# The 16 remaining tokens of a recurrent mixer as one packed block-diagonal system, with its inverse in the turns of the big one

## The reference, cut to what matters

```python
def rwkv7_scan(r, decay, k, v, kk, a):
    def step(S, inp):
        r_t, w_t, k_t, v_t, kk_t, a_t = inp
        sa = jnp.einsum('bhvk,bhk->bhv', S, -kk_t)
        S = (S * w_t[:, :, None, :]
             + sa[..., None] * (kk_t * a_t)[:, :, None, :]
             + v_t[..., None] * k_t[:, :, None, :])
        o = jnp.einsum('bhvk,bhk->bhv', S, r_t)
        return S, o
```

## Time and profile before

| | us |
|---|---|
| three timed runs | 1591.23, 1601.34, 1601.97 |
| their median | 1601.34 |
| the profiled execution's own time | 1596.85 |
| its span in the profile | 1595.1 |
| mean granted clock of TensorE in it | 0.99 |

### The profile page before, as it was taken

One profiled execution on the slowest core, in us unless ns is written; L12 is line 12 of the kernel. 1 busy time (PEld: TensorE's weight loads), 2 busy tenths in 40 slices (PEclk: granted clock), 3 DMA queues, 4 the chain that ended last, 5 costly groups with the idle time before them and its releaser, 6 DMA issues. The chain is left out here.

```text
span 1595.1 us, 33719 instructions
## 1 busy us (share of the span) xinstructions
PE 1521.0 (95%) x14204; PEld 1465.0 (92%) x14204; DVE 1042.8 (65%) x1584; ACT 741.1 (46%) x1025; POOL 61.0 (4%) x82
## 2 busy tenths in 40 slices
PE   5999999999999999999999999999998998899997
PEld 5999998999999898999989998999998987799996
DVE  7999647888763868454488855545445677565644
ACT  2555434696212754444456022566334345466532
POOL 0121100000110000110000100000000000000000
PEclk9999999999999999999999989999999999999999
DMA  9899754543221455555433001344543331235551
GB/s 367 312 331 342 271 195 163 178 166 119 78 86 59 167 207 217 202 194 187 176 127 132 10 29 31 129 167 175 176 168 114 133 115 71 79 137 202 190 187 51
DMA packets 39200, 256.86 MB, mean 161 GB/s; under 512 B 4259, under 2 KB 5668, under 8 KB 9892
## 3 DMA queue, kind: packets, MB, share of 16 engines
q1 hardware_dynamic: 37492, 251.07, 43.6%
q10 hardware_dynamic: 1584, 3.97, 0.6%
HBM read 251.87 MB, written 3.15 MB: 160 GB/s over the span
## 5 line engine op out<-in xcount | busy, mean ns | idle before, releaser
L472 DVE TENSOR_TENSOR w_lo<-raw,w_hi 128x2048 fp32r<-128x2048 f32 (+2 forms) x203 | 456.3, 2248 | 388.4 <-ACT w_hi L464 387.8
L572 PE MATMUL bank<-x_hi,w_hi 128*128 128x256 f32 (+1 forms) x1826 | 519.2, 284 | 15.0 <-DVE w_lo L472 6.1
L464 ACT ACTIVATE w_hi<-raw 128x2048 fp32r<-128x2048 f32 (+2 forms) x203 | 382.0, 1882 | 303.0 <-PE bank L574 281.2
L574 PE MATMUL bank<-x_hi,w_lo 128*128 128x256 f32 (+1 forms) x1826 | 511.5, 280 | 0.0
L573 PE MATMUL bank<-x_lo,w_hi 128*128 128x256 f32 (+1 forms) x1826 | 511.0, 280 | 0.0
L572 PEld LDWEIGHTS bank<-x_hi,w_hi 128*128 128x128 f32 x1826 | 343.3, 188 | 22.7 <-issue 14.9
L573 PEld LDWEIGHTS bank<-x_lo,w_hi 128*128 128x128 f32 x1826 | 343.7, 188 | 0.9 <-issue 0.7
L574 PEld LDWEIGHTS bank<-x_hi,w_lo 128*128 128x128 f32 x1826 | 343.6, 188 | 0.0
L573 PE MATMUL bank<-mh_lo,w_hi 128*128 128x272 f32 (+1 forms) x512 | 144.4, 282 | 0.0
L572 PE MATMUL bank<-mh_hi,w_hi 128*128 128x272 f32 (+1 forms) x512 | 144.4, 282 | 0.0
L574 PE MATMUL bank<-mh_hi,w_lo 128*128 128x272 f32 (+1 forms) x512 | 144.4, 282 | 0.0
(11 more groups left out here) (611 smaller groups left out, 2512.4 us busy)
## 6 DMA issues: line engine op xcount, KB each, us to landing
raw<-in_stream SPq DMA_DIRECT2D x227, 1024.0 KB, 4.8
raw<-in_stream SPq DMA_DIRECT2D x8, 768.0 KB, 4.0
gate_store<-stage ACTq DMA_DIRECT2D x8, 256.0 KB, 2.3
raw<-in_stream SPq DMA_DIRECT2D x4, 512.0 KB, 3.4
h<-in_h ACTq DMA_DIRECT2D x1, 1088.0 KB, 9.8
zt<-gate_store SPq DMA_DIRECT2D x1, 1024.0 KB, 5.7
gate<-gate_store SPq DMA_DIRECT2D x1, 1024.0 KB, 7.9
out<-h SPq DMA_DIRECT2D x8, 128.0 KB, 1.8
```

The costliest lines, as they stand in the source:

```text
L464: nc.scalar.activation(w_hi[:, s_at % 2, 0:kt], raw[:, r_at % RING, 0:kt], ACT.Copy).then_inc(hi_done, 1)
L472: nc.vector.tensor_tensor(w_lo[:, s_at % 2, 0:kt], raw[:, r_at % RING, 0:kt], w_hi[:, s_at % 2, 0:kt].bitcast(F32), ALU.subtract).then_inc ...
L572: nc.tensor.matmul(out, hi, xh[:, k0 + k, 0:L], start=start, stop=False)
L574: mm = nc.tensor.matmul(out, lo, xh[:, k0 + k, 0:L], start=False, stop=stop)
```

## The change

The end chunk's heads are packed. Of each half (partitions 0 to 63 and 64 to 127) the four heads' 16 tokens form one 64x64 system, block-diagonal in blocks of 16 (`ends_*`, tiles of 128x64). A gram of all four heads is one 64x64 product, and masks (`ends_before`, `ends_upto`) keep the blocks. The four levels of its inverse stand in the turns of the big inverse: `begin_ends` behind `grow` of turn 1, then for levels 1 to 3 `ends_p` at the start of turns 2 to 4, `ends_masked`, `ends_y` and, ahead of the big `grow`, `ends_grown`. The instance `small` is gone from the steps, and step 2 becomes `last_step`. TURN_BUSY goes from 4 to 3, SOLVE_BUSY from 3 to 7, and one call of SOLVE_BUSY products is left in the steps; fillers of turns change places (slabs in even ones, bonus in odd ones). `pool_products(3)` moves into step 0. In step 1 the state's products for the outputs go ahead of the wait for the solution, and the new state waits for these alone (`state_read`). `begin_out` now does two tiles in the last step and six behind it. On ACT, `outputs(0)` and `square(0)` come behind `pool_out(2)` and the pooling tiles' high part; on DVE the second w_lo split moves from step 1 to step 0, and `centred(0)`, `variance(0)` shift.

```diff
-TURN_BUSY, FIRST_TURN_BUSY, SOLVE_BUSY, END_BUSY, OUT_BUSY, MIX_BUSY = 4, 12, 3, 8, 14, 26
+TURN_BUSY, FIRST_TURN_BUSY, SOLVE_BUSY, END_BUSY, OUT_BUSY, MIX_BUSY = 3, 12, 7, 8, 14, 26
...
                 shifted(None, 6, 0)
+                dve.wait_ge(q["sh_done"], VAL2 + 1)
+                nc.vector.tensor_copy(v_ends[:].rearrange("p (k n) -> p k n", k=RW), v_t[:, :, 2 * P:T2]).then_inc(q["v_ends"], 1)
                 split_lo(dve, following(S["ev_u"], None, 2, 0, 0, False))
...
+                def ends_of(xs, bank, c0):
+                    for n, x in enumerate(xs):
+                        for ps in HALVES:
+                            mm = nc.tensor.matmul(banks[bank][ps, c0 + 64 * n:c0 + 64 * (n + 1)], ends_left[ps, x % 2], grams[x][1][ps, :, end_cols], start=True, stop=True)
                     mm.then_inc(m["gr2"], 1)
+
+                def ends_p(l):
+                    pe.wait_ge(m["e_x"], l)
+                    for ps in HALVES:
+                        mm = nc.tensor.matmul(banks[0][ps, ENDS_P], ends_a[ps, 0], joined(ends_x[ps], l, 0)[:, 0], start=True, stop=True)
+                    mm.then_inc(m["e_p"], 1)
...
-                        small.products_p(pe, 2 * c)
                         idle_slab(1, SOLVE_BUSY)
...
+                    if c:
+                        pe.wait_ge(m["oo_out"], 1)
+                        for k in range(RW):
+                            mm = nc.tensor.matmul(banks[5][:, k * P:(k + 1) * P], r_t[:, k, cols], state_bd[:, k], start=k == 0, stop=False, skip_group_check=True)
+                        mm.then_inc(m["state_read"], 1)
...
+                def last_step():
+                    pe.wait_ge(m["st_out"], 2)
+                    pe.wait_ge(m["gr2_out"], 1)
+                    for ps in HALVES:
+                        for k in range(RW):
+                            nc.tensor.matmul(banks[0][ps, 0:64], ends_kk[ps, 64 * k:64 * (k + 1)], state_bd[ps, k, ps], start=k == 0, stop=False)
+                        mm = nc.tensor.matmul(banks[0][ps, 0:64], ends_ak[ps, 0], v_rw[ps, 2, 0:64], start=False, stop=True)
+                    mm.then_inc(m["rr"], 1)
+                    begin_out(BEGUN[0:2])
+                    pe.wait_ge(m["e_x"], 4)
+                    pe.wait_ge(m["rr_out"], 3)
+                    for ps in HALVES:
+                        mm = nc.tensor.matmul(banks[1][ps, 0:64], ends_y_t[ps, 0], rhs_r[ps, 0:64], start=True, stop=True)
+                    mm.then_inc(m["ww"], 1)
...
+                    begin_out(BEGUN[2:8])
...
                     else:
+                        if l - 1 in ENDS_LEVELS:
+                            ends_p(l - 1)
                         if l % 2:
+                            bonus_product((l + 1) // 2)
+                        else:
                             idle_slab(0, TURN_BUSY)
-                        else:
-                            bonus_product(1 + l // 2)
                         big.products_p(pe, l)
...
+                    if l - 1 in ENDS_LEVELS:
+                        ends_y(l - 1)
                     if l:
                         big.products_y(pe, l)
...
-                ends_of((0, 1))
+                ends_of((1, 2, 3), 2, 0)
                 big.cross_y(pe)
                 pool_products(1)
-                ends_of((2, 3))
-                idle_slab(1, SOLVE_BUSY)
                 big.wait_whole(pe)
                 step_of(0)
                 step_of(1)
-                begin_out(BEGUN[0:4])
-                step_of(2)
+                last_step()
...
+                def begin_ends():
...
+                    link(dve, "dve", nc.vector.tensor_scalar(ends_a[:, 0], banks[0][:, ENDS_A], -1.0, None, ALU.mult))
+                    nc.vector.tensor_copy(joined(ends_y_t[:], 0, 0), joined(eye, 0, 0))
+                    link(dve, "dve", nc.vector.tensor_tensor(joined(ends_y_t[:], 0, 1), joined(ends_a[:], 0, 1), mask, ALU.mult))
+                    link(dve, "dve", nc.vector.tensor_tensor(joined(ends_y_t[:], 0, 1), joined(eye, 0, 1), joined(ends_y_t[:], 0, 1), ALU.subtract))
+                    nc.vector.transpose(ends_x[:, 0], ends_y_t[:, 0]).then_inc(m["e_x"], 1)
...
+                    if l - 1 in ENDS_LEVELS:
+                        ends_grown(l - 1)
+                    big.grow(dve, l)
+                    if l == 1:
+                        begin_ends()
```

More of the change, by code:

```diff
@@ L2645, in step_of @@
                         pe.wait_ge(m["kb_out"], 4)
[L2646 to L2653, removed]
+                        pool_products(2, 3)
+                        for k in range(3):
+                            first_outputs(k)
@@ L2695, in _ @@
                         pe.wait_ge(act_took, 2 + S["ev_u"].t0 + 2)
+                        pe.wait_ge(m["e_left"], 1)
+                        ends_of((0,), 0, ENDS_A.start)
                         big.products_p(pe, l, (0,))
@@ L2808, in _ @@
                 nc.scalar.activation(x_hi[:, 4:8], z_pool, ACT.Copy).then_inc(m["z_hi"], 1)
+                outputs(0)
+                square(0)
                 root(0)
                 outputs(1)
-                small.diagonal(act)
                 square(1)
@@ L2931, in normed, with ends_masked, ends_grown @@
                     nc.vector.tensor_tensor(heads8(dev[0:C, c]), heads8(dev[0:C, c]), rstd, ALU.mult).then_inc(m["nrm"], 1)
+                def begin_ends():
+                    mask = const("levels").rearrange("p (l f n) -> p l f n", l=LEVELS, f=2)[:, 0, 1][:, None, :, None]
+                    eye = const("eyes")[:, None, :]
+                    dve.wait_ge(m["gr2"], 1)
+                    link(dve, "dve", nc.vector.tensor_scalar(ends_a[:, 0], banks[0][:, ENDS_A], -1.0, None, ALU.mult))
[3 more added lines that the diff above has]
+                    nc.vector.transpose(ends_x[:, 0], ends_y_t[:, 0]).then_inc(m["e_x"], 1)
+                def ends_masked(l):
+                    half, b = QUAD // 2, 1 << l
+                    mask = const("levels").rearrange("p (l f n) -> p l f n", l=LEVELS, f=2)[:, l, 0].rearrange("p (n b) -> p n b", b=b)[:, None]
+                    link(dve, "dve", nc.vector.memset(ends_prod[:], 0.0))
+                    dve.wait_ge(m["e_p"], l)
+                    product = banks[0][:, ENDS_P].rearrange("p (h n b) -> p h n b", h=1, b=b)
+                    nc.vector.tensor_tensor(joined(ends_prod[:], l, 0), product, mask, ALU.mult).then_inc(m["e_pd"], 1)
+                def ends_grown(l):
+                    part = joined(ends_y_t[:], l, 1)
+                    dve.wait_ge(m["e_yu"], l)
+                    link(dve, "dve", nc.vector.tensor_tensor(part, part, banks[1][:, ENDS_P].rearrange("p (h n b) -> p h n b", h=1, b=1 << l), ALU.subtract))
+                    nc.vector.transpose(ends_x[:, 0], ends_y_t[:, 0]).then_inc(m["e_x"], 1)
                 for n, x in enumerate((nb_t[:], k_t)):
@@ L2937, in _ @@
                 nc.vector.tensor_tensor(r_t, r_t, log_g[:], ALU.mult).then_inc(m["decayed"], 1)
+                for n, x in enumerate((nb_t[:], k_t)):
+                    ins = nc.vector.tensor_copy(ends_left[:, n].rearrange("p (k n) -> p k n", k=RW), x[:, :, end_cols])
+                ins.then_inc(m["e_left"], 1)
                 for c in range(2):
@@ L2957, in _ @@
                 rescaled(1)
[L2958 removed]
+                dve.wait_ge(m["e_kz"], 1)
+                nc.vector.tensor_copy(ends_kk[:].rearrange("p (k n) -> p k n", k=RW)[:, :, 0:TAIL], kk_t[:, :, end_cols])
                 dve.wait_ge(m["gr2"], 2)
[L2960 to L2964 removed]
@@ L2966, in small_p @@
-                def small_p(l):
-                    small.zero(dve, nc.vector, l)
-                    small.masked(dve, l)
+                for n, (dst, mask) in enumerate(((ends_ak, "ends_before"), (ends_rb, "ends_upto"), (ends_rk, "ends_upto"))):
+                    ins = nc.vector.tensor_tensor(dst[:, 0], banks[2][:, 64 * n:64 * (n + 1)], const(mask), ALU.mult)
+                ins.then_inc(m["gr2_out"], 1)
                 for c in range(2):
                     right_side(c)
-                    small_p(2 * c)
```

168 lines of the change are left out of this document (69 added, 99 removed).

## The result

The changed kernel took 1611.6 us (median of 20 runs, 1600.2 to 1616.7), the kernel before in the same comparison 1594.2 (20 runs, 1586.1 to 1613.2). The ratio on record is 1.0098, with a 95% interval of 1.0078 to 1.0119 (the medians divided give 1.011): slower, where 1582 was forecast and 1595 was the upper end. The profiled execution took 1612.4 us, of which 1610.6 are span.

What follows compares the result with a forecast made beforehand. PE, busy 95% of the span, was taken as the bound, with a PE-DVE loop setting the turns. Profiled 1596.85 us, +3.5 before step 0, -18.3 from there to the next stage gave 1582.0; range 1574 to 1595.

Steps and rivals of the forecast that it cites:

- Turn 2: Start of the big inverse's second turn: PE's new wait for DVE's ends_x delays the big product, +2.5 us (+1.5 to +3.2).
- the sum: Whole kernel: profiled 1596.85 us, +3.5 up to step 0, -18.3 from there to the next stage, giving 1582.0.
- step 0: First step after the turns: products, seven slabs, transposes and state at full clock, 11.3 us where it was 13.8.
- Rival (c): Turns: clock falls in the wait and isn't given back while only 64-row products run; +24, 1606 us; chance 0.06.
- only cover: Turns: the four slabs at 901.97 merely fill PE's time while DVE's loop sets the turn of 6.89 us.
- Rival (b): Turn 2: PE waits and the clock falls for half a turn; +2 to +4, about 1585 to 1586 us; chance 0.14.
- The turns: Turns 2 to 4: small subtraction and transpose lengthen DVE's loop; 7.3 or 7.5 us a turn, +0.6, +0.4, +0.5.
- Rival (d): Turns: small inverse's DVE operations meet full queues, +6 not +3.5, and steps gain only 13.3; 1589.6 us; chance 0.10.
- The steps: Step 0 to the next stage at full clock: 38.5 us where it was 56.8, so -18.3.
- rival (a): Steps: the clock falls there all the same, PE's chain losing about 5 us; 1587 us; chance 0.22.
- the gain from alternating halves: Step 2: overlapping both halves would make the first ten products 0.7 us instead of 1.4; not taken in the forecast.

Runs made afterwards that it cites:

- the version with the product behind: The changed kernel with the small product (ends_x, ends_a) behind the big one in turns 2 to 4, so without the wait: 1576.3 us, ratio 0.9908.
- the run with five copies: The kernel before plus only a PE wait ahead of turn 2 for five small DVE copies behind turn 1's second transpose: 1625.9 us, ratio 1.0223.
- the gap covered: The changed kernel with 21 more slab products in turn 2 ahead of the wait for ends_x: 1579.2 us, ratio 0.9918.
- the run with 40 slabs: The changed kernel with 40 slab products instead of 3 at the start of turn 4: 1597.2 us, ratio 1.0031.

## Why the prediction was wrong

*The step that failed* is "Turn 2", the +2.5 us for the first new wait, together with the price of the clock in it. The wait was seen, in its place, with its releaser, and nearly in its size: idle 2.69 us for a forecast of about 2.4, a delay of 2.9 us by itself for 2.5. What failed is the sum's premise that everything behind it keeps its durations, so that the fall of the clock stood in the sum at nothing. From the second product to step 0 it took 63.91 us where the forecast's terms give 37.67, +26.2, and step 0 took 16.58 us (959.74 to 976.32) for a forecast 11.3, +5.3. Together that is 31.5 us; the profiled execution missed the 1582.0 by 30.4. Rival (c) named this mechanism with a price of +24, though it took the half clock to end with the 64-row products, where it went on through most of step 0. It got a chance of 0.06.

*The argument against rival (c)* was that the same turns ran at full clock with four slabs a turn, and that PE is busy again right after the gap. Both are true, and neither bears on the question. That full clock is kept in a stretch says nothing of whether it is given back there; 75.00 us of 75 busy at 0.50 show that it isn't. And the slabs, "only cover" in the prediction, were no spare help: without them and with 0.73 us of idle time in their place the clock goes.

*Rival (b) and the page behind it.* The Trainium skill, "TensorE: Matmul & The Clock Gate", Part 1, section "What's actually happening", has the clock fall after an idle spell and return after a busy one. The first half fits the gaps, though the idle spells here were as short as 1.63 us and, in turn 4, 0.73; it doesn't fit the dip of step 1 before, where PE was busy for 5.00 of 5 us. The second half doesn't fit these turns: PE had no idle time for 75 us and no clock came back. The measurement decides; the page should not have stood behind "the gap could cost this and no more".

*The turns.* 7.3 to 7.5 us were forecast; the version without the gap has 7.54 and, over three turns, 7.41 (895.52 to 917.75). From the second product to step 0 it takes 37.37 us; the forecast's own terms give 37.12 + 0.6 + 0.4 + 0.5 + 0.15 - 1.1 = 37.67. Rival (d) is out.

*The steps.* In the version with the product behind: 38.5 forecast, 37.99 measured, step 0 in 10.97 for 11.3, and no half clock. The 18.3 us to be won there were real, and rival (a) is not seen. Part of them is luck: about 5 were the half clock of the one execution the sum was made against, and the run with five copies shows that steps 0 and 1 can keep full clock with their small products too. Step 0 needs no slabs for it either. One price was read from unlike rows: the gain from alternating halves compared 64-column records (0.07) with 32-column ones (0.033). The ten 64x64 products of step 2, half after half, took 1.1 us in the changed kernel (988.50 to 989.63) for the 1.4 of the sum.

*The sum.* Without the clock's fall but with the delay, the forecast was 1582.0, 14.8 under the kernel before; the run that is just this, the gap covered, gave 1579.2, 14.5 under the kernel before in its comparison (1593.7). So the failure is one mechanism, not several terms. The change is not quite confined to one stage, as the prediction has it: TURN_BUSY also sets the fillers of a loop in the first block, four before and three now. The clock line shows no dip there. The version with the product behind the big one, at 1576.3, beats both kernels: 0.9908 of before, and some 2% under the changed one.

*Open* is why behind the wait of 0.50 us in turn 2 the clock held and behind 0.73 in turn 4 it did not: length and place differ, and no run separates them. Open too is why the clock came back at 942 in one kernel with a gap and at 972 in another, and what makes it fall in the steps of the kernel before. Nor was it tried how few wide products in a turn would give the clock back.

## What to carry to other kernels

Before pricing a new wait on PE at its length, look at what PE runs behind it: if that is a long stretch of narrow products, the wait can cost the clock for the whole stretch, here 35 us in all for a wait of 2.7. Put a small product that depends on a fresh result behind the large one that doesn't, in the order of the queue; where it must stand first, cover the wait. And judge fillers by taking them out once: three slab products at each of two places, which look like waste, were worth 23 us.

## What the hardware showed that was not expected

- The lower clock lasted 75 us with PE busy for all of it, some 64 of them (895.83 to 959.74) under products mostly of 64 rows and 32 to 128 columns, and ended among 128-row products: in step 0 of the changed kernel at 972.2, and in the run with 40 slabs within 6.7 us of them. In the kernel before with five copies it lasted 48 us and ended right behind 128x128 products.
- The same narrow products hold full clock when nothing is idle between them (22 us, busy 21.92). Holding and winning back are two things.
- Behind a wait of 1.63 us among narrow products the clock went; behind 1.48 us between 128-row products of 256 and 272 columns, and 0.78 us between ones of 64 columns, it stayed at 1.00.
- In the kernel before, the clock fell with PE busy for 5.00 of 5 us, behind short 16x16 products. In the run with five copies the clock stayed at 1.00 through the same products (945 to 990), so they are not enough by themselves.
